# Order of VectorE's and ScalarE's work in the experts of a hybrid layer: turned inner rows ahead of weight parts

## The chip, the cores and the metric

The kernel runs on one core of one Trainium2 chip. The metric is the device time of one execution in microseconds (us), as the median of several runs; the kernel before takes 1356.16 us (three runs, 1355.96 to 1356.65). The core's five engines each work off an instruction stream of their own and meet through semaphores: PE (TensorE, matrix products), DVE (VectorE), ACT (ScalarE), POOL (GpSimd), and SP (SyncE), which here only issues DMAs.

## What is computed

One layer with 1024 tokens and 16 meta tokens: a mixer (convolutions and a gated delta rule), then a mixture of 32 experts, and a last norm. The change is in the experts alone. There, each token goes to two experts, and an expert computes, in float32:

```python
def expert_block(args):
    xb, e = args                                   # up to 128 token rows of 1024
    hid = jax.nn.silu(xb @ w_gate[e]) * (xb @ w_up[e])   # 1024 -> 512, twice
    return hid @ w_down[e]                         # 512 -> 1024
...
w_top, e_top = lax.top_k(jax.nn.softmax(exp_logits, axis=-1), TOP_K)   # TOP_K = 2
out = jnp.zeros((T + 1, D), xf.dtype).at[row_tok].add(y_rows * row_w[:, None])
out = rms_norm(h + out, final_norm_w)
```

## The kernel before, in words

Each expert takes one block of 128 gathered token rows; a loop for experts that get more than 128 rows stands behind the experts and its body isn't entered here. A product in float32 precision is made of three matrix products in a faster format: each operand x is split into a high part (x rounded) and a low part (x minus the high part), and high times high, high times low and low times high are summed in PSUM (`product`, lines 585 to 587). So each of an expert's three matrices (m = 0 gate, 1 up, 2 down; 128 x 4096 values each) goes through the same steps: SP loads it into its one raw buffer `w_raw` (2 MB, `load_unit`, line 379), ACT writes the high part `w_hi` in two halves (`split`, line 731), DVE writes the low part `w_lo` in two halves (`split`, line 949), and once both are through, SP loads the same matrix of the next expert (`refill`, line 418). The raw, high and low buffers exist once per matrix.

The activations take a second path. POOL gathers the expert's rows by an indirect DMA (line 1135). PE turns them by eight transposes (`turn`, line 576), ACT and DVE write their high and low parts `xgT_hi`, `xgT_lo` (`turned`, lines 747 and 1007). After the gate product ACT computes its silu (line 752), after the up product DVE multiplies the two into the inner rows `hid` (`hidden`, line 1014). PE turns these by four transposes (`hid_turn`, line 604), ACT and DVE write the parts of the turned inner rows, `hidT_hi` and `hidT_lo` (`down_in`, lines 756 and 1018), and with these PE can start the down product. ACT scales its result (`y_out`, line 765) and POOL scatters it by an indirect DMA (line 1141).

PE works with a lag of one: in step e it does the lower half of gate(e), `hid_turn(e - 1)`, the upper half of gate(e), down(e - 1), `turn(e + 1)`, up(e). The gate, up and down products are 24 matrix products each. The order on each engine is written out by hand, one stream each in `tail_tensor`, `tail_scalar`, `tail_vector`, `tail_sync` and `tail_pool`; no scheduler moves anything. The steps e = 1 to 30 are `expert(...)` on PE, ACT and DVE; the first and the last ones stand outside the loops (Fori) of two experts per turn. `down_in(e)` on ACT waits for `ht_e` (four transposes done), on DVE for `hta_done` (ACT's part done); PE waits for `hte_done` in front of down, and in `gate_up` for `hi_done` and `lo_done`, matrix by matrix and half by half. SP's refills come in the order up(e), gate(e + 1), down(e), each with a wait for both halves of that raw buffer.

Of the kernel before, what the change touches and what calls it, by code (L numbers as in the profile page):

```python
# [43 lines left out]
E = 32  # L44
# [72 lines left out]
def layer_kernel(nc, x, consts, par, mix_w, wt, w_out, ffn_w, fin_w, w_gate, w_up, w_down, out):  # L117
    ctx = ExitStack()
    with ctx:
# [552 lines left out]
        def tail_scalar(act):  # L672
# [48 lines left out]
                if t == 4:  # L721
                    rows_turned(4)

            def split(e, m):

                act.wait_ge(w_sem[m], e * 16 + 16)
                if not isinstance(e, int) or e > 0:
                    act.wait_ge((g_done, u_done, d_done)[m], e)
                for b in range(2):
                    half = slice(b * WU // 2, (b + 1) * WU // 2)  # L730
                    nc.scalar.activation(w_hi[m][:, half], wraw[m][:, half], ACT.Copy).then_inc(hi_done[m], 1)  # L731

# [4 lines left out]
            nc.scalar.activation(tk[4], tk[4], ACT.Exp).then_inc(r_act, 1)  # L737

            split(0, 0)
            act.wait_ge(h_stored, 16 * NT)  # L740
            act.wait_ge(x2_stored, 16 * NT)
            split(0, 1)

            def turned(e, p):
                act.wait_ge(xt_e, e + 1)
                for b in range(2):
                    nc.scalar.activation(xgT[p][0][:, 4 * b:4 * b + 4, :], bank[5 + b][:, :].rearrange("p (k n) -> p k n", k=4),
                                         ACT.Copy).then_inc(xte_act, 1)

            def silu_gate(e, p):  # L750
                act.wait_ge(g_done, e + 1)
                nc.scalar.activation(gs[p], bank[p][:, :], ACT.Silu).then_inc(silu_e, 1)

            def down_in(e):
                act.wait_ge(ht_e, e + 1)
                nc.scalar.activation(hidT[0], bank[7][:, :].rearrange("p (k n) -> p k n", k=4), ACT.Copy).then_inc(hta_done, 1)

            def y_out(e, p, col=None, before=None, banks=(3, 4)):
                act.wait_ge(d_done, e + 1)
                if before is not None:  # L760
                    act.wait_ge(scattered[p], before * 16)
                c = e if col is None else col
                w = wtab[:, c:c + 1] if isinstance(c, int) else wtab[:, bass.ds(c, 1)]
                for b in range(2):
                    m = nc.scalar.activation(ysb[p][:, b * 512:(b + 1) * 512], bank[banks[b]][:, :], ACT.Copy, scale=w)  # L765
                m.then_inc(y_act, 1)

            turned(0, 0)
            silu_gate(0, 0)
            split(1, 0)  # L770
            turned(1, 1)
            split(0, 2)

            def expert(e, p, before):

                split(e, 1)
                down_in(e - 1)
                silu_gate(e, p)
                split(e + 1, 0)
                y_out(e - 1, 1 - p, None, before)  # L780
                turned(e + 1, 1 - p)
                split(e, 2)

            act.wait_ge(tables, 2)
            act.wait_ge(zero_sent, 16)
            expert(1, 1, None)
            expert(2, 0, None)
            with act.Fori(1, E // 2 - 1) as j:
                expert(j * 2 + 1, 1, j)
                expert(j * 2 + 2, 0, j)  # L790
# [32 lines left out]
        def tail_vector(dve):  # L823
# [120 lines left out]
            def split(e, m, halves=(0, 1)):  # L944

                for b in halves:
                    half = slice(b * WU // 2, (b + 1) * WU // 2)
                    dve.wait_ge(hi_done[m], e * 2 + b + 1)
                    nc.vector.tensor_tensor(w_lo[m][:, half], wraw[m][:, half], w_hi[m][:, half].bitcast(F32),  # L949
                                            ALU.subtract).then_inc(lo_done[m], 1)  # L950
# [53 lines left out]
            def turned(e, p):  # L1004
                for b in range(2):
                    dve.wait_ge(xte_act, e * 2 + b + 1)
                    nc.vector.tensor_tensor(xgT[p][1][:, 4 * b:4 * b + 4, :],  # L1007
                                            bank[5 + b][:, :].rearrange("p (k n) -> p k n", k=4),
                                            xgT[p][0][:, 4 * b:4 * b + 4, :].bitcast(F32), ALU.subtract).then_inc(xte_dve, 1)

            def hidden(e, p):
                dve.wait_ge(silu_e, e + 1)
                dve.wait_ge(u_done, e + 1)
                nc.vector.tensor_tensor(hid, bank[2][:, :], gs[p], ALU.mult).then_inc(hid_done, 1)

            def down_in(e):
                dve.wait_ge(hta_done, e + 1)
                nc.vector.tensor_tensor(hidT[1], bank[7][:, :].rearrange("p (k n) -> p k n", k=4), hidT[0].bitcast(F32),  # L1018
                                        ALU.subtract).then_inc(hte_done, 1)
# [2 lines left out]
            split(0, 1)  # L1022
            split(1, 0)
            turned(1, 1)
            split(0, 2)
            hidden(0, 0)

            def expert(e, p):

                split(e, 1, [0])  # L1030
                down_in(e - 1)
                split(e, 1, [1])
                split(e + 1, 0)
                turned(e + 1, 1 - p)
                split(e, 2, [0])
                hidden(e, p)
                split(e, 2, [1])

            expert(1, 1)
            with dve.Fori(1, E // 2 - 1) as j:  # L1040
                expert(j * 2, 0)
                expert(j * 2 + 1, 1)
# [8 lines left out]
            tt(hot31, row(iota[:, 0:128], NT), per(tok31, 128), ALU.is_equal).then_inc(f_hot, 1)  # L1051
            split(E - 1, 2, [0])
            hidden(E - 1, 1)
            split(E - 1, 2, [1])
            down_in(E - 1)

            def over(j):
                dve.wait_ge(scattered[0], (j + E // 2) * 16)
# [670 lines left out]
        def _(dve):  # L1729
# [297 lines left out]
            for h in range(H):  # L2027
                mixer(h, h == H - 1)
            tail_vector(dve)


# [94 lines left out]
```

## Time and profile before

| | |
|---|---|
| median of 3 runs | 1356.16 us |
| profiled execution, its own time | 1354.1 us |
| its span, first to last instruction | 1352.3 us |
| mean granted TensorE clock | 0.985 of full |
| PE, DVE, ACT busy | 1299.9, 906.0, 719.3 us |
| HBM read, written | 260.11 MB, 29.36 MB |
| experts, first turn to last down product | about 725 to 1317 us of the span |

The page of the profile gives the engines' busy time in all, in 40 slices, the chain of work that ended last and the costliest groups of instructions. Matrix products are pipelined and their ends are modelled, so a product of 0.39 us starts every 0.23 us; what counts for PE is the distance between starts. A PE row of a full wait shows it behind the row, as "[idle before <-releaser]". The views cited below are the busy time by stretch, the waits by who waited for whom, and the timeline of single instructions, in which neighbours of one kind are merged (x2).

### The profile page before, as it was taken

How to read it: one execution, taken by the hardware profiler on the slowest of the kernel's cores; microseconds unless marked ns; L12 is line 12 of the kernel's file. 1: busy time of each engine (PE TensorE's matmuls, PEld its weight loads, DVE VectorE, ACT ScalarE, POOL GpSimd, SP SyncE). 2: the span in 40 equal slices, each digit the busy share in tenths (PEclk: the TensorE clock that was granted, in tenths of full speed). 3: DMA queues.
4: the chain of work that ended last, by engine and by line, in shares of the span. 5: the costliest groups of instructions: out<-in, count | busy, mean ns of one | idle time of the engine just before them, and what ended most of it. 6: DMA issues, size and time to landing. Idle time of an engine off the chain costs nothing.

```text
span 1352.3 us, 19015 instructions
## 1 busy us (share of the span) xinstructions
PE 1299.9 (96%) x7544; PEld 1132.6 (84%) x7544; DVE 906.0 (67%) x1060; ACT 719.3 (53%) x919; POOL 154.5 (11%) x144
## 2 busy tenths in 40 slices
PE   6999999999999999989997999999999999999997
PEld 5989998999899989968886788888888888888874
DVE  6753556355635563624247888888898888888967
ACT  7351335123512351524215787878778878787744
POOL 0020111011201120520001011111101111111000
PEclk9989999999999999999997999999999999999999
DMA  7100000001100100306415999999999999999968
GB/s 204 48 16 27 22 32 32 16 32 32 32 17 32 32 32 1 125 12 255 170 78 216 345 369 367 380 382 386 394 372 391 376 374 382 379 376 386 372 268 329
DMA packets 38047, 273.56 MB, mean 202 GB/s; under 512 B 8147, under 2 KB 8403, under 8 KB 25700
## 3 DMA queue, kind: packets, MB, share of 16 engines
q1 hardware_dynamic: 28340, 251.67, 49.1%
q0 software_dynamic: 9216, 16.80, 3.3%
q10 hardware_dynamic: 432, 4.27, 0.8%
q8 instruction: 42, 0.69, 0.2%
q14 instruction: 17, 0.14, 0.0%
HBM read 260.11 MB, written 29.36 MB: 214 GB/s over the span
## 4 chain that ended last, share of the span: by engine, by line
PE 90%; DVE 5%; ACT 2%; issue 1%; DMA 1%; SPq 0%; DVEq 0%; POOLq 0%
PE bank L585 13%; PE bank L587 13%; PE bank L586 13%; PE bank L1285 8%; PE bank L1287 8%; PE bank L1286 8%; PE bank L1412 3%; PE bank L1410 3%; PE bank L474 2%; PE bank L476 2%; PE bank L475 2%; PE bank L576 2%; DVE arena L1801 1%; PE bank L604 1%; PE bank L1298 1%
## 5 line engine op out<-in xcount | busy, mean ns | idle before, releaser
L949 DVE TENSOR_TENSOR w_lo<-w_raw,w_hi 128x2048 fp32r<-128x2048 f32 x192 | 433.7, 2286 | 54.1 <-ACT w_hi L731 54.1
L731 ACT ACTIVATE w_hi<-w_raw 128x2048 fp32r<-128x2048 f32 x192 | 357.5, 1917 | 19.8 <-DMA w_raw<-in_w_up 11.7
L1285 PE MATMUL bank<-xn_hi,p_hi 128*128 128x364 f32 (+1 forms) x672 | 229.2, 341 | 2.1 <-DVE p_lo L1736 2.1
L1287 PE MATMUL bank<-xn_hi,p_lo 128*128 128x364 f32 (+1 forms) x672 | 217.0, 323 | 0.0
L1286 PE MATMUL bank<-xn_lo,p_hi 128*128 128x364 f32 (+1 forms) x672 | 216.5, 322 | 0.0
L585 PE MATMUL bank<-w_hi,xgT_hi 128*128 128x512 f32 x512 | 206.9, 404 | 2.9 <-DVE xgT_lo L1007 2.9
L587 PE MATMUL bank<-w_hi,xgT_lo 128*128 128x512 f32 x512 | 201.7, 394 | 0.0
L586 PE MATMUL bank<-w_lo,xgT_hi 128*128 128x512 f32 x512 | 201.1, 393 | 0.0
L1285 PEld LDWEIGHTS bank<-xn_hi,p_hi 128*128 128x128 f32 x672 | 127.9, 190 | 2.9 <-DVE p_lo L1736 2.5
L1286 PEld LDWEIGHTS bank<-xn_lo,p_hi 128*128 128x128 f32 x672 | 128.0, 190 | 0.3
L1287 PEld LDWEIGHTS bank<-xn_hi,p_lo 128*128 128x128 f32 x672 | 127.5, 190 | 0.0
L585 PEld LDWEIGHTS bank<-w_hi,xgT_hi 128*128 128x128 f32 x512 | 97.2, 190 | 22.2 <-issue 3.6
L587 PEld LDWEIGHTS bank<-w_hi,xgT_lo 128*128 128x128 f32 x512 | 96.8, 189 | 21.2
L586 PEld LDWEIGHTS bank<-w_lo,xgT_hi 128*128 128x128 f32 x512 | 97.3, 190 | 19.0
L585 PE MATMUL bank<-w_hi,hidT_hi 128*128 128x512 f32 x256 | 103.3, 403 | 3.8 <-DVE hidT_lo L1018 2.1
L1641 ACT ACTIVATE arena<-bank 104x416 f32<-104x416 f32 (+1 forms) x72 | 28.4, 459 | 143.4 <-PE bank L1408 143.4
L586 PE MATMUL bank<-w_lo,hidT_hi 128*128 128x512 f32 x256 | 100.3, 392 | 0.0
L587 PE MATMUL bank<-w_hi,hidT_lo 128*128 128x512 f32 x256 | 100.3, 392 | 0.0
L1141 POOL DMA_INDIRECT y_rows<-arena x31 | 31.2, 1006 | 496.9 <-ACT arena L765 496.9
L2002 DVE SCALAR_TENSOR_TENSOR arena<-arena,bank 128x128 f32<-128x128 f32 x40 | 14.0, 349 | 84.9 <-PE bank L1450 84.9
L585 PEld LDWEIGHTS bank<-w_hi,hidT_hi 128*128 128x128 f32 x256 | 48.4, 189 | 24.3 <-DVE hidT_lo L1018 8.0
L765 ACT ACTIVATE arena<-bank,arena 128x512 f32<-128x512 f32 x62 | 39.3, 685 | 53.4 <-PE bank L587 53.4
(253 smaller groups left out, 2018.8 us busy)
## 6 DMA issues: line engine op xcount, KB each, us to landing
w_raw<-in_w_down SPq DMA_DIRECT2D x32, 2048.0 KB, 9.3
w_raw<-in_w_gate SPq DMA_DIRECT2D x31, 2048.0 KB, 11.0
w_raw<-in_w_up SPq DMA_DIRECT2D x31, 2048.0 KB
p_raw<-in_w_tiles SPq DMA_DIRECT2D x28, 512.0 KB, 3.3
arena<-y_rows SPq DMA_DIRECT2D x8, 1024.0 KB, 14.2
arena<-in_tokens SPq DMA_DIRECT2D x10, 416.0 KB
w_out_raw<-in_w_out SPq DMA_DIRECT2D x4, 1024.0 KB, 8.1
arena<-in_tokens SPq DMA_DIRECT2D x8, 512.0 KB, 4.4
```

The costliest lines, as they stand in the source:

```text
L585: nc.tensor.matmul(out, xh, wh, start=start, stop=False)
L586: nc.tensor.matmul(out, xh, wl, start=False, stop=False)
L587: return nc.tensor.matmul(out, xl, wh, start=False, stop=stop_)
L731: nc.scalar.activation(w_hi[m][:, half], wraw[m][:, half], ACT.Copy).then_inc(hi_done[m], 1)
L765: m = nc.scalar.activation(ysb[p][:, b * 512:(b + 1) * 512], bank[banks[b]][:, :], ACT.Copy, scale=w)
L949: nc.vector.tensor_tensor(w_lo[m][:, half], wraw[m][:, half], w_hi[m][:, half].bitcast(F32), ALU.subtract).then_inc(lo_done[m], 1)
L1141: nc.gpsimd.indirect_dma_start(out=y_dram, out_offset=bass.IndirectOffsetOnAxis(ap=stab[:, c:c + 1], axis=0), in_=ysb[p], in_offset=None, ...
L1285: nc.tensor.matmul(out[:, 0:n], p_hi[slot][:, k, :], hi, start=(k == 0), stop=False)
L1286: nc.tensor.matmul(out[:, 0:n], p_hi[slot][:, k, :], lo, start=False, stop=False)
L1287: m = nc.tensor.matmul(out[:, 0:n], p_lo[slot][:, k, :], hi, start=False, stop=(k == KD - 1))
L1410: m = nc.tensor.matmul(o, tI[0:C, c, :], zz[0:C, c, :], start=True, stop=True)
L1412: m = nc.tensor.matmul(o, lM[0:C, c, :], rT[0:C, c, :], start=True, stop=True)
```

## The change

Four edits in two streams. On ACT, in each step of the experts 1 to 30, `down_in(e - 1)` moves between the two halves of the up matrix's high part; it stood behind both. On DVE, in the same steps, `down_in(e - 1)` moves ahead of both halves of the up matrix's low part; it stood between them. At the start, `hidden(0, 0)` moves ahead of the low parts of down(0) on DVE. At the end, `down_in(31)` moves ahead of the second half of the low part of down(31) on DVE. The arithmetic is the same. In the diff, the hunks down to `silu_gate` are ACT's, those behind them DVE's.

```diff
-            def split(e, m):
+            def split(e, m, halves=(0, 1)):
...
-                for b in range(2):
+                for b in halves:
...
             def expert(e, p, before):
 
-                split(e, 1)
+                split(e, 1, [0])
                 down_in(e - 1)
+                split(e, 1, [1])
                 silu_gate(e, p)
...
             turned(1, 1)
+            hidden(0, 0)
             split(0, 2)
-            hidden(0, 0)
 
             def expert(e, p):
 
-                split(e, 1, [0])
                 down_in(e - 1)
-                split(e, 1, [1])
+                split(e, 1)
...
             split(E - 1, 2, [0])
             hidden(E - 1, 1)
+            down_in(E - 1)
             split(E - 1, 2, [1])
-            down_in(E - 1)
```

On DVE, this is the piece from the turned rows of expert 1 to the low part of gate(2): `w_lo_67`, `_68`, `_69` are the low parts of gate, up and down, the line with `arena<-bank,arena` is `hidden`. Before:

```order
L1007 TENSOR_TENSOR xgT_lo<-bank,xgT_hi 128x512 x2
L949 TENSOR_TENSOR w_lo_69<-w_raw_63,w_hi_66 128x2048 x2
L1014 TENSOR_TENSOR arena<-bank,arena 128x512
L949 TENSOR_TENSOR w_lo_68<-w_raw_62,w_hi_65 128x2048
L1018 TENSOR_TENSOR hidT_lo<-bank,hidT_hi 128x512
L949 TENSOR_TENSOR w_lo_68<-w_raw_62,w_hi_65 128x2048
L949 TENSOR_TENSOR w_lo_67<-w_raw_61,w_hi_64 128x2048 x2
```

and the same piece of the changed kernel, whose lines are numbered one higher:

```order
L1008 TENSOR_TENSOR xgT_lo<-bank,xgT_hi 128x512 x2
L1015 TENSOR_TENSOR arena<-bank,arena 128x512
L950 TENSOR_TENSOR w_lo_69<-w_raw_63,w_hi_66 128x2048 x2
L1019 TENSOR_TENSOR hidT_lo<-bank,hidT_hi 128x512
L950 TENSOR_TENSOR w_lo_68<-w_raw_62,w_hi_65 128x2048 x2
L950 TENSOR_TENSOR w_lo_67<-w_raw_61,w_hi_64 128x2048 x2
```

`hidden` passes two weight halves of the first expert's down matrix, and `hidT_lo` passes one half of the up matrix; the latter is the same in every step up to expert 30.

On ACT, this is one step, from the down matrix's high part (`w_hi_66`) to that of the gate matrix (`w_hi_64`); `w_hi_65` is the up matrix's, line 752 the silu. The piece of the difference:

```order
 L731 ACTIVATE w_hi_66<-w_raw_63 128x2048 x2
-L731 ACTIVATE w_hi_65<-w_raw_62 128x2048 x2
-L756 ACTIVATE hidT_hi<-bank 128x512
+L731 ACTIVATE w_hi_65<-w_raw_62 128x2048
+L756 ACTIVATE hidT_hi<-bank 128x512
+L731 ACTIVATE w_hi_65<-w_raw_62 128x2048
 L752 ACTIVATE arena<-bank 128x512
```

The high part of the turned inner rows passes one half of the up matrix; the second half now stands between it and the silu. PE's and SP's streams are unchanged.

## Rows read from the trace of the kernel before

**Rows 1.** Busy time by stretch: from:to, length, busy (count), clock, DMA share, GB/s.
```profile
749.50:753.00 3.50, 3.48 (x11) 2.90 (x12) 3.46 (x3) 2.29 (x3) 0.00 (x0) 0.54 1.01 360
...
900.00:950.00 50.00, 49.88 (x237) 40.93 (x236) 43.47 (x29) 40.38 (x34) 6.08 (x6) 1.00 1.00 386
...
1301.00:1304.00 3.00, 3.00 (x14) 2.46 (x14) 0.00 (x0) 2.97 (x4) 0.97 (x1) 1.00 1.03 422
```

**Rows 2.** Waits from 760 to 1290 us: total us, times, longest.
```profile
ACT w_hi L731 <- DMA w_raw<-in_w_up: 9.2, 13, 1.0
...
PEld bank L585 <- issue: 7.1, 14, 0.5
PEld bank L585 <- DVE hidT_lo L1018: 5.6, 15, 0.4
```

**Rows 3.** Timeline of PE: start, us, operation; three steps, experts 13, 14 and 30.
```profile
985.54 0.60 PE L604 MATMUL bank<-arena 128*128 128x128 f32 x4
...
994.21 0.39 PE L587 MATMUL bank<-w_hi,hidT_lo 128*128 128x512 f32 x1
...
1003.52 0.60 PE L604 MATMUL bank<-arena 128*128 128x128 f32 x4
...
1007.00 0.47 PE L585 MATMUL bank<-w_hi,hidT_hi 128*128 128x512 f32 x1
...
1012.32 0.39 PE L587 MATMUL bank<-w_hi,hidT_lo 128*128 128x512 f32 x1
...
1292.18 0.60 PE L604 MATMUL bank<-arena 128*128 128x128 f32 x4
...
1300.60 0.39 PE L587 MATMUL bank<-w_hi,hidT_lo 128*128 128x512 f32 x1
```

**Rows 4.** Timeline of DVE in the second of these steps.
```profile
1001.67 4.48 DVE L949 TENSOR_TENSOR w_lo<-w_raw,w_hi 128x2048 fp32r<-128x2048 f32 x2
1006.07 0.68 DVE L1018 TENSOR_TENSOR hidT_lo<-bank,hidT_hi 128x512 fp32r<-128x512 f32 x1
1006.67 2.28 DVE L949 TENSOR_TENSOR w_lo<-w_raw,w_hi 128x2048 fp32r<-128x2048 f32 x1
1009.36 4.50 DVE L949 TENSOR_TENSOR w_lo<-w_raw,w_hi 128x2048 fp32r<-128x2048 f32 x2 [0.41 <-ACT w_hi L731]
1014.71 1.29 DVE L1007 TENSOR_TENSOR xgT_lo<-bank,xgT_hi 128x512 fp32r<-128x512 f32 x2 [0.85 <-ACT xgT_hi L747]
```

**Rows 5.** Timeline of ACT in the same step.
```profile
1001.05 3.72 ACT L731 ACTIVATE w_hi<-w_raw 128x2048 fp32r<-128x2048 f32 x2 [0.47 <-PE bank L587]
1004.67 0.58 ACT L756 ACTIVATE hidT_hi<-bank 128x512 fp32r<-128x512 f32 x1
1006.92 0.60 ACT L752 ACTIVATE arena<-bank 128x512 f32<-128x512 f32 x1 [1.67 <-PE bank L587]
...
1012.93 1.27 ACT L765 ACTIVATE arena<-bank,arena 128x512 f32<-128x512 f32 x2 [1.79 <-PE bank L587]
```

**Rows 6.** Timeline of SP's queue: issue of the load of the next up matrix.
```profile
1009.18 0.33 SPq L379 DMA_DIRECT2D w_raw<-in_w_up  x1
```

**Rows 7.** Timeline at the start of the experts, four rows of DVE, ACT and PE.
```profile
744.38 4.48 DVE L949 TENSOR_TENSOR w_lo<-w_raw,w_hi 128x2048 fp32r<-128x2048 f32 x2
...
747.60 3.71 ACT L731 ACTIVATE w_hi<-w_raw 128x2048 fp32r<-128x2048 f32 x2 [2.48 <-DMA w_raw<-in_w_up]
...
749.52 0.88 PE L604 MATMUL bank<-arena 128*128 128x128 f32 x4 [2.54 <-DVE arena L1014]
...
759.86 1.03 PE L576 MATMUL bank<-arena 128*128 128x128 f32 x8
```

**Rows 8.** Timeline at the last expert's down product.
```profile
1307.15 2.28 DVE L949 TENSOR_TENSOR w_lo<-w_raw,w_hi 128x2048 fp32r<-128x2048 f32 x1
...
1307.98 0.60 ACT L756 ACTIVATE hidT_hi<-bank 128x512 fp32r<-128x512 f32 x1 [2.08 <-PE bank L604]
...
1310.09 0.79 PE L585 MATMUL bank<-w_hi,hidT_hi 128*128 128x512 f32 x1 [2.14 <-DVE hidT_lo L1018]
```

## The prediction

> **What bounds the kernel now.** I read the busy time by stretch first. In the experts PE is busy 49.88 of 50 us at full clock, DVE 43.5 and ACT 40.4 [rows 1]: PE sets the pace, and DVE and ACT have 10 to 20% to spare. The DMA share is 1.00 there too, at 386 GB/s, so a second candidate for the bound has to be weighed below. Next the waits: in 530 us PE waits for nothing but 29 short stops in front of the first down product, 15 put down to DVE's `hidT_lo` and 14 to "issue" [rows 2]. One per step, so the reader is to look at one step of each kind.
>
> The timeline of PE shows what a stop costs. From the four transposes of the inner rows to the last down product it takes 994.21 - 985.54 = 8.67 us in the one kind and 1012.32 - 1003.52 = 8.80 in the other; in the step of expert 30 the same instructions take 1300.60 - 1292.18 = 8.42 [rows 3]. That step differs in just one thing: there DVE's stream already has `down_in` ahead of both halves of the up matrix. So the stops cost 0.25 and 0.38 us, the restart of the row of products included.
>
> Why PE stops is seen on DVE and ACT. ACT works through both halves of the up matrix's high part from 1001.05 and writes `hidT_hi` at 1004.67 [rows 5]; DVE by then is in a half of the up matrix and comes to `hidT_lo` at 1006.07 [rows 4], ready at 1006.75, while PE wants it at about 1006.7 (1003.52, the transposes, and 12 products at 0.23) and starts at 1007.00 [rows 3]. DVE is the late one, by less than one weight half.
>
> **The change part by part.** Steps 1 to 30, DVE and ACT. PE's transposes start at 1003.52 and take 0.60, so the rows are turned at 1004.12 [rows 3]. ACT has the first half behind it at 1001.05 + 1.9 = 1002.95, waits, writes `hidT_hi` from 1004.15 to 1004.73 and does the second half to 1006.6; the silu began at 1006.92, behind an idle time of 1.67, which becomes 0.3 [rows 5]. DVE ends the down matrix's half at 1001.67 + 2.2 = 1003.9 (two halves take 4.40 from 1001.67 to 1006.07), waits 0.9 us for ACT and has `hidT_lo` at 1004.76 to 1005.4 [rows 4]. PE wants it at 1006.7: 1.3 us to spare, and the stop goes. Term 1: 15 x 0.25 + 14 x 0.38 = 9.1 us. The pace per expert falls by 0.31.
>
> What hides the rest. DVE's two up halves end at 1005.36 + 4.40 = 1009.8 in place of 1006.67 + 2.28 = 8.95, that is 0.8 later; the gate halves end at 1014.2 in place of 1009.36 + 4.50 = 1013.9; then comes `xgT_lo`, for which ACT now is ready at 1014.71 - 0.31 = 1014.4 [rows 4]. DVE's idle times of 0.41 and 0.85 there are the cover, and about 0.2 is left of them. PE's up product needs the up parts only behind its transposes, some 1.0 us after 1012.32 [rows 3]: 3 us to spare. If that cover went, DVE would give the rest of its delay to the down matrix's first half, not to PE at once.
>
> SP's loads are the price of the move. The next up matrix is issued at 1009.18 [rows 6], with the end of the low part; now at 1010.0. It is wanted when PE ends the up product, 1001.05 + 18.0 = 1019.1 before, 0.3 earlier after: the window shrinks from 9.9 to 8.8 us. Already now 13 of 29 such loads end after ACT could start, by 0.7 us on the average (9.2 / 13) and by 1.0 at most [rows 2]. The lateness then is bounded by 0 and by 1.0 + 0.8 + 0.3 = 2.1 us. On the new order ACT can be 1.2 us late before `hidT_hi` moves (1002.95 against 1004.15), and 1.3 more before `hidT_lo` reaches PE's 1006.7: 2.5 us in all, above the upper bound. A late silu and gate matrix come out of the 1.79 us ahead of line 765 [rows 5]. The new order thus tolerates the very lateness that it makes. For several late loads in a row I take 1 us off the sum, near the end 0 of its bounds (0 to the 9.1 of the term), since no row shows a load later than 1.0.
>
> Can the DMA engines go faster at all? An expert moves 386 GB/s x 18.0 us = 6.95 MB; where loads were queued deeply, 422 GB/s flowed at a share of 1.03 [rows 1], and at that rate it takes 16.5 us, below the 17.7 that PE would then need. So the share of 1.00 isn't a rate at its limit, and I take the loads as not binding. The Trainium skill, "DMA: Bandwidth & Descriptors", the section on specifications, puts the HBM limit of one core at about 358 GB/s; by it the loads would bind already and the first term would be zero. Both rows stand above that figure, so here the trace decides against it.
>
> The start. `hidden(0, 0)` stood behind two halves that start at 744.38 [rows 7]; it can now have their place, since PE's stop of 2.54 us ends with it, and PE would do the transposes at 749.52 - 2.54 = 746.98. Its next 12 products take about 3.2 us more (3.48 from 1003.52 to 1007.00, without the stop) [rows 3], to 750.2. The down product then waits for ACT: the up matrix lands at 747.60, a half takes 1.85, `hidT_hi` 0.6, `hidT_lo` 0.6 (durations as in [rows 4, 5]): 750.7. Down takes 8.42 - 3.2 + 0.2 = 5.4 to its end, 756.2, where the transposes of the next expert started at 759.86 [rows 7]. Term 2: 3.6 us; part of it is the clock, which was 0.54 of full from 749.5 to 753.0, behind the stop [rows 1]: of its two levels, 1.2 and 2.4 GHz, mostly the lower. Bounds: 2.5 (the clock falls all the same) and 3.7. I take 3.4. What is late next is the gate matrix of expert 2 and those behind it; they are issued with DVE's low parts, whose place moves by no more than 0.7 us.
>
> The end. `down_in(31)` no longer waits behind the half at 1307.15. ACT has `hidT_hi` at 1307.98 + 0.60 = 1308.6; DVE followed at 1307.15 + 2.20 = 1309.35 [rows 8]. Term 3: 0.75 us. The half that is passed ends at 1311.5, and PE needs it 12 products after its new start at 1309.3, at 0.23 or 0.43 us each, so after 1312. Cover: 0.5 us.
>
> Sum: 9.1 + 3.4 + 0.75 - 1.0 = 12.2 us. The profiled execution took 1354.1 us, so 1341.9; the median of the runs stands 2.1 above that execution, which makes 1344.0.
>
> **The rivals.** First, the loads do pace the experts. For it: the share of 1.00, and 13 late loads [rows 1, 2]. Against it: 422 GB/s [rows 1], and the step at 1001 us has its stop though ACT waited there for PE and not for a load [rows 5]. Then term 1 is gone and 4.2 us from start and end stay: 1352.0. If what the start gains is given back to the loads too, nothing stays: 1356.
>
> Second, the stops put down to "issue" are PE's own. In the step of 1003.52 `hidT_lo` is ready 0.25 us before the product starts, in the other kind 0.05. If 0.25 is what PE takes there in any case, 14 x 0.27 = 3.8 us of term 1 stay: 1347.8. Against it: the step of expert 30 has no stop at all [rows 3], but its stream isn't in the loop.
>
> Third, slower: the up load, issued 0.8 us later, is behind a queue that has run dry. Its place is [rows 6], its price up to 0.8 us per step in which the engines stand empty, and it decides once the load is over 2.5 us late (above) or once the empty time eats the difference between 16.5 and 17.7 us. With a third of the steps hit beyond that, and the gain of term 1 gone: 10 x 0.8 = 8 against 4.2: 1360; with all of them 1375.
>
> **How the numbers follow.** Forecast 0.62 (1341.5 to 1347), PE's own stops 0.13 (1346 to 1350), the loads as pace with start and end kept 0.12 (1350 to 1353.4), nothing left 0.05, slower 0.08. A measurement of this kernel tells 0.2%, 2.7 us, from no change. Faster than 1353.4: 0.87; within: 0.05; slower: 0.08. The forecast case could go below 1341.5 if the restart is cheaper than in the step of expert 30, so the range is 1341 to 1353; it leaves out 0.13 above and little below. The predicted time is 1344.0.
>
> **What would show it.** In the profile after: no waits of PE in front of the down product from 760 to 1290; from the transposes to the last down product 8.4 us in both kinds of step; `hidT_lo` starting about 1.3 us ahead of PE's need, with a DVE wait of 0.9 for ACT's line 756 in each step; ACT's idle time before the silu at 0.3; an expert at 17.7 us; more waits for the up matrix, none above 2.1 us; the first stop at the inner rows of expert 0 gone. The forecast is wrong if an expert still takes 18.0 us (then see whether a load or an "issue" ends PE's wait), or if ACT's waits for the up matrix exceed 2.5 us.

## The result and the profile after

The changed kernel takes 1344.61 us (median of 5 runs, 1341.84 to 1348.22) beside 1355.96 us before (5 runs, 1353.25 to 1356.65): a ratio of 0.9919, interval 0.9902 to 0.9937. Measured again later, beside other versions, it took 1345.39 us, a ratio of 0.9911 (0.9893 to 0.9930). The profiled execution took 1344.94 us, with a span of 1343.1, 9.2 less than before.

The busy time by stretch of the kernel after (columns as in [rows 1]) shows PE without an idle instant in the middle of the experts, at a DMA share of 0.99 beside 1.00 before:

```profile
900.00:950.00 50.00, 50.00 (x239) 41.56 (x238) 44.08 (x29) 40.31 (x35) 7.58 (x6) 1.00 0.99 388
```

The waits of the kernel after, from 760 to 1290 us (total us, times, longest), answer [rows 2]:

```profile
ACT w_hi L731 <- DMA w_raw<-in_w_up: 55.9, 30, 3.2
DVE hidT_lo L1019 <- ACT hidT_hi L756: 34.3, 30, 3.0
ACT w_hi L731 <- DMA w_raw<-in_w_gate: 28.9, 29, 1.7
...
ACT arena L752 <- PE bank L587: 4.6, 14, 0.4
PEld bank L585 <- DVE hidT_lo L1019: 2.6, 5, 1.3
PEld bank L585 <- issue: 1.6, 4, 0.8
...
PE bank L585 <- DVE hidT_lo L1019: 1.2, 2, 0.8
```

Two things have changed places. PE's 29 stops (12.7 us of waiting) are down to 11 (5.4 us), and ACT, which waited 13 times for an up matrix, now does so 30 times, for 1.9 us on the average and 3.2 at most, and 29 times for a gate matrix, which it had done twice.

One step of the kernel after, PE's timeline (answering [rows 3]), then DVE's ([rows 4]), ACT's ([rows 5]) and SP's ([rows 6]):

```profile
998.67 0.60 PE L604 MATMUL bank<-arena 128*128 128x128 f32 x4
...
1001.88 0.39 PE L585 MATMUL bank<-w_hi,hidT_hi 128*128 128x512 f32 x1
...
1007.09 0.39 PE L587 MATMUL bank<-w_hi,hidT_lo 128*128 128x512 f32 x1
```

```profile
999.94 0.69 DVE L1019 TENSOR_TENSOR hidT_lo<-bank,hidT_hi 128x512 fp32r<-128x512 f32 x1 [0.83 <-ACT hidT_hi L756]
1000.54 8.90 DVE L950 TENSOR_TENSOR w_lo<-w_raw,w_hi 128x2048 fp32r<-128x2048 f32 x4
1009.49 1.29 DVE L1008 TENSOR_TENSOR xgT_lo<-bank,xgT_hi 128x512 fp32r<-128x512 f32 x2
```

```profile
996.89 1.92 ACT L731 ACTIVATE w_hi<-w_raw 128x2048 fp32r<-128x2048 f32 x1 [1.15 <-DMA w_raw<-in_w_up]
999.30 0.60 ACT L756 ACTIVATE hidT_hi<-bank 128x512 fp32r<-128x512 f32 x1 [0.49 <-PE bank L604]
...
1002.08 0.60 ACT L752 ACTIVATE arena<-bank 128x512 f32<-128x512 f32 x1 [0.37 <-PE bank L587]
```

```profile
1005.26 0.33 SPq L379 DMA_DIRECT2D w_raw<-in_w_up  x1
```

From the transposes to the last down product it takes 1007.09 - 998.67 = 8.42 us, as in the step of expert 30 before. `hidT_lo` is ready at 1000.63, 1.2 us ahead of its use; the silu has 0.37 us of idle time left of 1.67; DVE does its four weight halves without a break (both idle times of [rows 4] are used up); and the up load is issued 6.6 us behind the transposes, where it was 5.7 (1009.18 against 1003.52).

Where the 9.2 us come from follows from a few rows of PE. Of before (first gate product, the transposes of expert 1, those of expert 31, the last down product):

```profile
728.66 0.76 PE L585 MATMUL bank<-w_hi,xgT_hi 128*128 128x512 f32 x1 [1.50 <-DVE xgT_lo L1007]
...
768.94 0.60 PE L604 MATMUL bank<-arena 128*128 128x128 f32 x4
...
1307.29 0.66 PE L604 MATMUL bank<-arena 128*128 128x128 f32 x4 [0.85 <-DVE arena L1014]
...
1316.80 0.39 PE L587 MATMUL bank<-w_hi,hidT_lo 128*128 128x512 f32 x1
```

and of after, with the transposes of expert 30 and the first down product of it too:

```profile
729.59 0.76 PE L585 MATMUL bank<-w_hi,xgT_hi 128*128 128x512 f32 x1 [1.50 <-DVE xgT_lo L1008]
...
767.48 0.60 PE L604 MATMUL bank<-arena 128*128 128x128 f32 x4
...
1283.81 0.60 PE L604 MATMUL bank<-arena 128*128 128x128 f32 x4
...
1288.02 0.50 PE L585 MATMUL bank<-w_hi,hidT_hi 128*128 128x512 f32 x1 [0.84 <-DVE hidT_lo L1019]
...
1300.09 0.66 PE L604 MATMUL bank<-arena 128*128 128x128 f32 x4 [0.85 <-DVE arena L1015]
...
1307.50 0.39 PE L587 MATMUL bank<-w_hi,hidT_lo 128*128 128x512 f32 x1
```

| piece | before | after | gain | predicted |
|---|---|---|---|---|
| first gate product to transposes of expert 1 | 40.28 | 37.89 | 2.4 | 3.4 |
| from there to the transposes of expert 30, 29 steps | 523.24 | 516.33 | 6.9 | 9.1 - 1.0 |
| to the transposes of expert 31 | 15.11 | 16.28 | -1.2 | 0 |
| to the last down product | 9.51 | 7.41 | 2.1 | 0.75 |
| ahead of the first gate product | 728.66 | 729.59 | -0.9 | 0 |

The sum is 9.3. The last row lies ahead of all that was changed and is no effect of the change: in the profile of the same kernel taken later (`e11_after_again`) the first gate product starts at 731.37. Two more pieces aren't the same in that profile: the 29 steps take 514.47 us in place of 516.33, and the step to the transposes of expert 31 takes 16.83 in place of 16.28.

### The profile page after: what moved, and what is told of

It reads as the page before. It is cut to its first block and busy times, and to the rows that moved or that the text cites. A ratio compares the mean times of both kernels' runs of the same rounds, so it can differ in the third digit from the quotient of the medians.

```text
span 1343.1 us, 19059 instructions
## 1 busy us (share of the span) xinstructions
PE 1292.4 (96%) x7544; PEld 1131.8 (84%) x7544; DVE 904.8 (67%) x1060; ACT 721.5 (54%) x919; POOL 179.4 (13%) x144
## 5 line engine op out<-in xcount | busy, mean ns | idle before, releaser
L1141 POOL DMA_INDIRECT y_rows<-arena x31 | 55.9, 1804 | 463.8 <-ACT arena L765 463.8
L1870 DVE TENSOR_TENSOR arena<-bank,arena 104x416 f32<-104x416 f32 (+1 forms) x72 | 34.6, 514 | 43.8 <-PE bank L1412 41.1
```

The source lines that it names most:

```text
L1141: nc.gpsimd.indirect_dma_start(out=y_dram, out_offset=bass.IndirectOffsetOnAxis(ap=stab[:, c:c + 1], axis=0), in_=ysb[p], in_offset=None, ...
L1870: m = nc.vector.tensor_tensor(zz[0:C, s], bmat(g)[0:C], lev[:, int(name[1:]), :].unsqueeze(1).to_broadcast([C, n, C]), ALU.mult)
```

## The experiments

Each was compared with the kernel before on the same chip; a ratio stands with its 95% interval.

**The edits one by one.** Five kernels take one or two of the four edits each. `e1_start` has the first one on DVE alone:

```diff
             turned(1, 1)
+            hidden(0, 0)
             split(0, 2)
-            hidden(0, 0)
```

> The kernel before with one edit of the four: hidden(0, 0) ahead of the low parts of down(0). Theory (each edit gives what its place shows in the two traces): PE's stop in front of the first inner transposes goes, experts 2 to 30 stay at 18.04 us each; 2 to 3 us faster, 1353 to 1354. Rival (what the start gains is given back, since the loads of the first experts are no earlier): the first transposes come 2.7 us earlier, but by expert 3 nothing is left; within 1 us of before.

Measured: 1355.82 us, ratio 0.9996 (0.9984 to 1.0009). The rival holds. PE's and ACT's timelines of this kernel show where it is given back:

```profile
746.16 0.60 PE L604 MATMUL bank<-arena 128*128 128x128 f32 x4
...
747.69 3.71 ACT L731 ACTIVATE w_hi<-w_raw 128x2048 fp32r<-128x2048 f32 x2 [3.25 <-DMA w_raw<-in_w_up]
...
751.30 0.58 ACT L756 ACTIVATE hidT_hi<-bank 128x512 fp32r<-128x512 f32 x1
...
752.86 0.66 PE L585 MATMUL bank<-w_hi,hidT_hi 128*128 128x512 f32 x1 [3.35 <-DVE hidT_lo L1018]
```

The transposes come earlier, but in ACT's old order the turned rows stand behind both halves of the up matrix of expert 1, which lands at 747.7, no earlier than before (747.60). The stop has only moved to the down product, and has grown from 2.54 us [rows 7] to 3.35; the clock fell behind it, as it had behind the other (0.58 of full in the stretch after):

```profile
753.00:757.00 4.00, 4.00 (x11) 3.17 (x12) 3.79 (x2) 3.71 (x2) 0.00 (x0) 0.58 1.00 385
```

`e2_steps` has the two edits in the steps, without start and end:

```diff
-                split(e, 1)
+                split(e, 1, [0])
                 down_in(e - 1)
+                split(e, 1, [1])
                 silu_gate(e, p)
...
-                split(e, 1, [0])
                 down_in(e - 1)
-                split(e, 1, [1])
+                split(e, 1)
                 split(e + 1, 0)
```

> The kernel before with the two edits in the steps of experts 1 to 30 alone (ACT's part of the turned inner rows between the halves of the up matrix, DVE's ahead of both). Theory: a step takes 17.73 instead of 18.04 us, 7 to 9 us faster in all, 1347 to 1349. Rival (part of the step's gain came from the start's head start, which the loads could not follow): steps above 17.85 us, less than 5 us faster.

Measured: 1348.09 us, 0.9939 (0.9921 to 0.9957). Nearly all of its steps take 17.73 us (from 769.63 to 1284.49 there are 29, of 17.75 on the average). So this is the larger part of the gain, and it doesn't need the head start.

`e3_dve` has the second of these two hunks alone, with ACT as before:

> DVE's reordering in the steps alone; ACT still does both up halves ahead of the turned inner rows. Theory (the loads of the up matrix, issued 0.8 us later, make ACT late by more than the old order of ACT can bear, some 0.7 us): stops of PE behind hidT_lo in many steps, a step between 17.8 and 18.1 us, 0 to 5 us faster than before. Rival A (DVE was the only late one and ACT's order is of no use): 17.73 us a step as with both, 7 to 9 us faster. Rival B (the later loads with the old order of ACT cost more than the stop): slower than before by over 2 us.

Measured: 1370.99 us (1365.07 to 1374.75), 1.0110 (1.0090 to 1.0131): slower, by 15 us. The theory of 0 to 5 us faster missed, and rival B holds. It is the prediction's third rival on one edit alone, as far as a later load makes the kernel slower; how the time is lost in the trace below isn't what that rival described (engines that stand empty, up to 0.8 us per step). The profiled execution is the fastest of the six, 1365.07 us; its steps take from 17.73 to 19.7 us, 18.30 on the average. The waits of this kernel from 760 to 1290 us, and one of its stops (ACT, DVE, PE):

```profile
DVE hidT_lo L1018 <- ACT hidT_hi L756: 65.3, 29, 3.8
ACT w_hi L731 <- DMA w_raw<-in_w_up: 38.8, 27, 2.9
...
PE bank L585 <- DVE hidT_lo L1018: 11.7, 15, 1.7
```

```profile
1064.39 3.71 ACT L731 ACTIVATE w_hi<-w_raw 128x2048 fp32r<-128x2048 f32 x2 [2.94 <-DMA w_raw<-in_w_up]
...
1068.01 0.57 ACT L756 ACTIVATE hidT_hi<-bank 128x512 fp32r<-128x512 f32 x1
...
1068.62 0.69 DVE L1018 TENSOR_TENSOR hidT_lo<-bank,hidT_hi 128x512 fp32r<-128x512 f32 x1 [3.85 <-ACT hidT_hi L756]
...
1069.36 0.50 PE L585 MATMUL bank<-w_hi,hidT_hi 128*128 128x512 f32 x1 [1.69 <-DVE hidT_lo L1018]
```

ACT starts on the up matrix 2.9 us late, does both halves, and only then the turned rows. DVE stands idle for 3.85 us meanwhile, so its low parts, and with them the next up load, are late as well: that load is issued at 1073.94, 9.6 us behind the transposes of this step (1064.31), where it was 5.7 in the kernel before.

`e4_act` has the first of the two hunks alone, with DVE as before:

> ACT's reordering in the steps alone; DVE still does one up half ahead of its part of the turned inner rows. Theory: hidT_hi comes about 0.5 us earlier, DVE comes to its part at the same time as before, the stops stay at 0.25 and 0.38 us and a step at 18.04 us; within 1 us of before. Rival (ACT's part was the late one in the steps with a late load): some of the stops shorter, 2 to 4 us faster.

Measured: 1356.62 us, 1.0004 (0.9993 to 1.0014): nothing, as the theory had it. ACT's edit is worth nothing by itself and yet, with the full loads, is what makes DVE's edit a gain.

`e5_end` has the last edit alone:

```diff
             hidden(E - 1, 1)
+            down_in(E - 1)
             split(E - 1, 2, [1])
-            down_in(E - 1)
```

> The kernel before with the last edit alone: down_in(31) ahead of the second half of down(31)'s low part on DVE. Theory: PE's last down product starts 0.75 us earlier, and where the shorter stop leaves the clock at its upper level its first products no longer take 0.43 us; 0.75 to 2.1 us faster, 1353.5 to 1355. Rival (the rows of y that the last stage loads set its start): the product ends earlier but the last stage doesn't; within 0.3 us of before.

Measured: 1354.04 us, 0.9992 (0.9982 to 1.0001), inconclusive as a time. In its trace the first product of down(31) starts 2.07 us behind the transposes where it was 2.80, as in the changed kernel. But the clock fell all the same, as it had in the kernel before:

```profile
1308.48 0.50 PE L585 MATMUL bank<-w_hi,hidT_hi 128*128 128x512 f32 x1 [1.41 <-DVE hidT_lo L1018]
...
1309.00:1312.00 3.00, 3.00 (x9) 2.31 (x9) 1.62 (x1) 0.00 (x0) 0.00 (x0) 0.54 1.00 404
```

The piece from the transposes of expert 31 to the last down product takes 9.05 us here, beside 9.51 before and 7.41 in the kernel after. So the part of the theory that puts the slow products down to the longer stop isn't borne out.

**Are the loads the cause?** Two kernels leave out half of each up matrix from expert 1 on (1 MB of an expert's 6 MB; the second half keeps expert 0's values), one as before, one as changed; a third does so for DVE's hunk alone. With that they don't compute the layer any more and serve for the time only:

```diff
-            eng.dma_start(wraw[slot], s).then_inc(w_sem[slot], 16)
+            part = slice(0, WU // 2 if slot == 1 and not (isinstance(e, int) and e == 0) else WU)
+            eng.dma_start(wraw[slot][:, part], s[:, part]).then_inc(w_sem[slot], 16)
```

> The kernel before, but from expert 1 on only the first half of each up matrix is loaded (the second half keeps expert 0's values), so 1 MB of 6 goes. Theory (PE's stops come from DVE's order and not from the loads): steps stay at 18.04 us, within 1.5 us of before. Rival (the loads pace the experts): the step falls by up to 2 us, tens of us faster.

Measured: 1355.38 us, 1.0005 (0.9992 to 1.0018), with a DMA share of 0.87 at 322 GB/s from 770 to 1270 us. Its waits show the same stops to the tenth of a us as [rows 2], without a single wait for a load:

```profile
PEld bank L586 <- issue: 7.1, 14, 0.5
PEld bank L586 <- DVE hidT_lo L1019: 5.6, 15, 0.4
```

So the loads did not pace the kernel before; the rival of a bound by the loads falls.

> The changed kernel with the same lighter loads (second half of the up matrices from expert 1 on not loaded). Theory: ACT's waits for the up matrix vanish, all 29 steps take 17.73 us and the step of expert 30 has no stop; 2 to 5 us faster than the changed kernel, 1340 to 1343, about 1.0% faster than before. Rival (the remaining stops aren't from late loads): the same time as the changed kernel.

Measured: 1341.58 us, 0.9905 (0.9890 to 0.9921). All 29 steps take 17.73 us, PE waits for nothing. As a time the difference from the changed kernel lies within the intervals.

> DVE's reordering in the steps alone, ACT in its old order, with the lighter loads. Theory (DVE's edit alone is slower because ACT, late for the load, does both up halves ahead of the turned inner rows): with loads in time the stops go and a step takes 17.73 us; 1345 to 1348, where the full loads gave 1371. Rival (the loss is in the order of the two engines itself, whatever the loads): still slower than before.

Measured: 1344.01 us, 0.9939 (0.9918 to 0.9960), and 17.73 us in every step. The same order of DVE and ACT that cost 15 us with the full loads wins some 8 to 11 with lighter ones. That settles the cause of `e3_dve`: it is the late load, not the order in itself.

**What is left to win.** `e8_last` treats on ACT the one step that the change left out:

```diff
-            split(E - 1, 1)
+            split(E - 1, 1, [0])
             down_in(E - 2)
+            split(E - 1, 1, [1])
             silu_gate(E - 1, 1)
```

> The changed kernel with the same reordering on ACT in the step of expert 30 to 31 too, which stands outside the loop and which the change left alone (down_in(30) between the halves of up(31)). Theory (the stop of 1.0 us in front of down(30) comes from the late load of up(31) and the old order there): the stop goes, 0.6 to 1.2 us faster than the changed kernel, 1343 to 1344. Rival (the load is later than the new order bears): no difference.

Measured: 1341.92 us, 0.9896 (0.9879 to 0.9914), beside 1345.39 of the changed kernel measured with it. The difference of 3.5 us is more than the theory's 0.6 to 1.2, and the intervals overlap. In its trace the stop in front of down(30) is gone (the first product 3.20 us behind the transposes, where the kernel after has 1288.02 - 1283.81 = 4.21):

```profile
1280.80 0.60 PE L604 MATMUL bank<-arena 128*128 128x128 f32 x4
...
1284.00 0.39 PE L585 MATMUL bank<-w_hi,hidT_hi 128*128 128x512 f32 x1
```

This step takes 15.10 us to the next transposes, where the changed kernel takes 16.28 and 16.83 in its two profiles. So the trace shows 1.2 to 1.7 us of the difference; the rest isn't shown to come from the edit.

`e9_halves` adds loads in two halves of 1 MB, each with its own semaphore:

```diff
-                sp.wait_ge(hi_done[m], b * 2)
-                sp.wait_ge(lo_done[m], b * 2)
-                load_unit(sp, e, m)
+                for h in range(2):
+                    sp.wait_ge(hi_done[m], b * 2 + (h - 1))
+                    sp.wait_ge(lo_done[m], b * 2 + (h - 1))
+                    load_unit(sp, e, m, [h])
...
-                act.wait_ge(w_sem[m], e * 16 + 16)
...
                 for b in halves:
+                    act.wait_ge(w_sem[m][b], e * 16 + (16 + 16 * b))
```

> The former kernel with each matrix loaded in two DMAs of 1 MB, each issued once its own half of the raw buffer has been split, and awaited by ACT half by half. Theory (the late loads are the whole rest): first halves are issued 2.2 us earlier and awaited on their own, the waits for the up matrix shrink below 0.5 us, no stops left, 1 to 3 us faster than the changed kernel, 1341 to 1343. Rival (twice the packets of half the size on busy engines): the engines move less per us, steps above 17.8 us, slower than the changed kernel.

Measured: 1340.61 us (1340.08 to 1342.17), 0.9885 (0.9868 to 0.9903): the fastest median of all, and some 2 us faster than expected beside the changed kernel. Its busy time from 770 to 1270 us, and two of its waits:

```profile
770.00:1270.00 500.00, 500.00 (x2371) 415.42 (x2370) 448.25 (x283) 404.89 (x339) 58.62 (x55) 1.00 1.00 386
```

```profile
ACT hidT_hi L759 <- PE bank L607: 36.0, 30, 1.2
...
DVE hidT_lo L1023 <- ACT hidT_hi L759: 24.5, 30, 0.8
```

No wait for a load is left in this stretch, ACT waits 1.2 us for PE's transposes in each step, as the prediction had it for loads in time, and all 29 steps take 17.73 us. Whether it beats `e8_last` can't be told: their intervals overlap. At the start it takes 36.6 us in place of 37.5 from the first gate product to the transposes of expert 1; at the end it happened to lose more, since the clock fell in its last down product and not in that of `e8_last` (8.96 and 7.43 us from the transposes).

> The changed kernel again, beside the two versions above on the same chip. Every theory: 1342 to 1347, 0.8% faster than before.

Measured: 1345.39 us (1341.71 to 1347.02), 0.9911 (0.9893 to 0.9930), as expected. Its steps lose much less than in the first profile (all but one at 17.73, the 29 together 0.2 us more than that), though ACT waits for an up matrix 30 times here too, for 1.5 us on the average and 2.9 at most. It has the stop in front of down(30) again, whose first product starts 4.80 us behind the transposes.

**What keeps the head start?** `e12_no_end` is the changed kernel without the last edit:

> The changed kernel without its last edit (down_in(31) again behind the second half of down(31)). Alone, the start edit gave 0.9996 and the end edit 0.9992 of before; the steps alone 0.9939, all four 0.9911 to 0.9919. Theory (the head start of the first edit is given back only under the old order of the steps, where DVE does a half of the up matrix, and so waits for its load, ahead of the turned inner rows; under the new order it is kept): 2 to 3 us faster than the steps alone, ratio to before 0.992, 1345 to 1346.5. Rival (the start gives nothing here either, and the difference comes from the end): ratio 0.9935 to 0.994, as the steps alone.

Measured: 1345.32 us, 0.9931 (0.9917 to 0.9945), between theory and rival; as a time it decides nothing. The trace does: from the first gate product to the transposes of expert 1 it takes 38.0 us, as in the kernel after (37.9), while `e2_steps`, without the first edit, takes 40.3, and `e1_start`, with that edit alone, 41.4. The head start of 2.3 us is there only with both.

The same trace shows something about the clock. Without the last edit, PE stands still for 2.14 us in front of down(31), as in the kernel before, and yet the clock stays up:

```profile
1301.11 0.50 PE L585 MATMUL bank<-w_hi,hidT_hi 128*128 128x512 f32 x1 [2.14 <-DVE hidT_lo L1019]
...
1301.00:1304.00 3.00, 2.89 (x13) 2.40 (x14) 0.27 (x2) 0.00 (x0) 0.00 (x0) 1.00 1.02 412
```

The piece from the transposes of expert 31 to the last down product takes 8.15 us here, 9.51 in the kernel before.

## Why the prediction held, and where it was off

**The bound and term 1.** That PE sets the pace and DVE's order makes the stops was right: `e6_before_light` shows both. That the stop costs 0.31 us per step, read from the one step that already had DVE's new order, was right to the hundredth: 18.04 became 17.73. That step stood outside the loop and so differed in more than the one thing that the prediction named; the steps at 8.42 us from transposes to last down product inside the loop (998.67 above) settle that. The 14 stops put down to "issue" went with the others, so the second rival falls.

**Late loads.** Here the prediction's bound failed, by its own sign of being wrong (waits for the up matrix above 2.5 us). I bounded the lateness of the up matrix by 2.1 us and put ACT's tolerance at 2.5; in the kernel after ACT waits 1.9 us on the average and up to 3.2, in 30 of 30 steps, three times above 2.5. The bound took the load's landing as shifted by its issue and added that to the largest lateness of one execution; it left out that gate loads got late too (29 of 29, 1.0 us). That these push the following loads is my reading; no run shows it by itself. The tolerance was a little smaller than thought: before, ACT began on the up matrix 2.47 us ahead of the transposes; after, the steps in which it began up to 0.24 us ahead of them (2.2 us later) take 17.73 us, and those in which it began 0.15 us ahead or later are longer, eight of the 29. In the profiled execution, 9.0 us (29 x 0.31) came out as 6.9. I had taken off 1.0; it was 2.1 there, but only 0.2 in the second profile of the same kernel, so that the size of the loss varies between executions and the 1.0 isn't refuted as an average.

**The step of expert 31, not counted.** ACT's stream keeps the old order there, and the up load that it waits for is now later: 1.2 us lost, 1.7 in `e11_after_again`. The prediction used this very step as its model of a step without stops and never asked what the later load does to it. `e8_last` shows the cause.

**The start.** 2.4 us in place of 3.4. The transposes came on time (at 747.91, of which 0.93 is the later first gate product), but I took the up matrix of expert 1 to land at 747.60, 18.9 us behind the first gate product; in the profile after, ACT could start on it at 749.48, 19.9 us behind, and the down product waits for it. That is the missing 1.0 us. It isn't a price of the change: in the eight other profiles that load these matrices in full and in one piece, four with the first edit and four without it (`e2_steps` to `e5_end`), this wait ended 19.2 to 20.0 us behind the first gate product. I had read it off an execution in which the load came early; what makes it vary is open. The prediction also said nothing of the condition under which this term exists: with the old order of the steps it is worth nothing (`e1_start`).

**The end.** 2.1 us in place of 0.75. The first product of down(31) came 0.73 us earlier, as worked out; the rest is the clock, and it is luck. Before, PE stood still for 0.85 and 2.14 us ahead of this product, and its first products took 0.63 us, at the lower of the two levels. After, it stood still for 0.85 and 1.41 us, and the stretch from 1302 to 1305 shows the clock at 1.00 of full:

```profile
1302.00:1305.00 3.00, 2.85 (x12) 2.36 (x13) 2.30 (x2) 0.00 (x0) 0.00 (x0) 1.00 1.01 393
```

I had kept the slow products in the sum, and it is tempting to say that the shorter stop saved them. The other traces don't bear that out. With the last edit, so behind the shorter stops, the clock fell in this product in three of six profiles (`e5_end`, `e7_after_light`, `e9_halves`); without it, behind the longer ones, it stayed up in two of eight (`e10_dve_light`, `e12_no_end`). From the transposes to the last down product it takes 7.4 us with the edit and 8.15 without where the clock stayed up, so the edit is worth 0.7 us. Where the clock fell, 1.4 us or more came on top, with the edit and without it. What decides on the fall isn't shown.

**The rivals.** The loads as pace: excluded for the kernel before. The slower case through the later up load: a later load does cost time, 15 us where ACT's edit is left out. The trace of `e3_dve` shows it lost through ACT's order; whether DMA engines that stand empty add to it isn't shown. The errors (2.1 - 1.0 too little, 1.2 not counted and 1.0 at the start against 1.35 at the end) add up to 2.0 us; with 0.9 lost ahead of the experts that makes 2.9 of the 3.0 by which the profiled execution stands above the 1341.9 forecast for it. Against the median of 1344.0, the measured 1344.61 owes some of its closeness to luck: I took the median to stand 2.1 above the profiled execution, as in the runs before, and it stood 0.3 below it. So the mechanism of the main term was right, and the closeness of the number is partly chance.

## What to carry to other kernels

Work that a busy engine waits for goes ahead of work with slack, but when that delays the release of a buffer, the next load is late, and the engine that waits for the load needs its own order changed first: one half of such a pair can be worth nothing and the other cost 15 us. Look at the steps outside the loop, which keep the old order and meet the new timing. Where a stop of PE can be compared with a step that lacks it, in the same trace, its price can be read off instead of estimated.

## What was not expected of the hardware

The same instructions behind the same stops of PE met the granted clock at its upper level in one execution and at its lower one in another: behind stops of 0.85 and 1.41 us it fell in three of six profiles, behind 0.85 and 2.14 us in six of eight. A difference of 1.4 us or more between two single profiles can be that and nothing else. Weights of 6 MB per 17.7 us were loaded at a share of 1.00 and 386 GB/s with no engine waiting for them (`e9_halves`), nearly the share and rate (0.99, 384 GB/s from 770 to 1270 us) at which the changed kernel waited for nearly every up load: the share doesn't tell whether loads are late, the waits do.
